# Key scores that follow the next block's queries, lists selected block by block, and keys kept in the place of the probabilities

## The reference

```python
q = (xc @ w_q).reshape(t, PEER_HEADS, 2, PEER_QDIM // 2)          # 1024 -> 2048 = 16 x 128
sc = jnp.einsum('thpc,hpnc->thpn', q, sub_keys)                   # 16 lists of 128 scores for a token
v_half, i_half = lax.top_k(sc, PEER_TOPK_HALF)                    # the best 16 of each list
cand = v_half[:, :, 0, :, None] + v_half[:, :, 1, None, :]        # 8 x 256 sums
top_s, pos = lax.top_k(cand, PEER_TOPK)                           # the best 16 of each: 128 experts a token
g = jax.nn.softmax(top_s, axis=-1)
act = jax.nn.gelu(jnp.einsum('thkd,td->thk', u_tab[expert], xc))
return jnp.einsum('thk,thkd->td', g * act, v_tab[expert])
```

## Time and profile before

| | |
|---|---|
| median of 3 executions | 2381.94 us (2380.4 to 2388.47) |
| profiled execution, its own time | 2383.69 us |
| its span in the profile | 2381.9 us, mean granted PE clock 0.877 |
| PE, DVE, ACT, POOL busy | 1820.2, 1430.4, 806.3, 638.4 us |
| gathers of the four feeds | 512 on POOL, from 222 us on |
| first route, PE | query blocks from 135.5 us |

### The profile page before, as it was taken

How to read it: one execution, slowest core, us unless ns; L and a number is a source line. 1 busy time by engine, 2 the same in 40 slices (tenths; PEclk the granted TensorE clock), 3 DMA queues, 4 the chain that set the end, 5 groups by cost and what they waited for, 6 DMA issues and landing times.

```text
span 2381.9 us, 21120 instructions
## 1 busy us (share of the span) xinstructions
PE 1820.2 (76%) x6754; PEld 1103.0 (46%) x6754; DVE 1430.4 (60%) x2933; ACT 806.3 (34%) x2074; POOL 638.4 (27%) x524
## 2 busy tenths in 40 slices
PE   6586877877777877777787776764786977987988
PEld 3473333623323362232445332653342445866976
DVE  2439845769665567965446896667566144554644
ACT  1211353233334423342432334212654123432532
POOL 0001423435333344443224453424452000000000
PEclk9597988889998998999888898887998975988999
DMA  8067988999999999999879998999896720442442
GB/s 290 20 236 279 406 323 335 419 421 421 378 419 396 338 422 421 406 392 421 320 259 412 420 421 340 421 421 420 341 421 264 252 103 36 177 194 100 178 161 102
DMA packets 106525, 744.79 MB, mean 313 GB/s; under 512 B 12848, under 2 KB 13744, under 8 KB 18352
## 3 DMA queue, kind: packets, MB, share of 16 engines
q0 software_dynamic: 73728, 536.90, 55.3%
q1 hardware_dynamic: 30240, 198.67, 21.8%
q10 hardware_dynamic: 2448, 7.87, 0.9%
HBM read 742.35 MB, written 1.05 MB: 312 GB/s over the span
## 4 chain that ended last, share of the span: by engine, by line
PE 41%; DMA 21%; DVE 21%; ACT 10%; issue 4%; DVEq 1%; POOL 1%; PEldq 1%; POOLq 0%; ACTq 0%; PEld 0%; SPq 0%
DMA sb_work<-in_peer_uv,sb_expert 18%; PE ps_acc L1270 11%; DVE sb_work L1234 6%; PE bank L434 4%; PE bank L1102 4%; PE bank L496 3%; PE bank L497 2%; PE bank L498 2%; PE bank L677 2%; DMA sb_wring<-in_peer_w_q 2%; DVE sb_x L1242 2%; ACT sb_probs L728 2%; PE ps_acc L1659 2%; PE ps_acc L498 1%; PE ps_acc L496 1%
## 5 line engine op out<-in xcount | busy, mean ns | idle before, releaser
L1270 PE MATMUL ps_acc<-sb_work,sb_diag 128*128 128x512 f32 x1532 | 800.3, 670 | 243.4 <-ACT sb_diag L1259 203.6
L2060 POOL DMA_INDIRECT sb_work<-in_peer_uv,sb_expert x512 | 636.0, 1242 | 1175.0 <-PE ps_acc L1270 590.6
L1234 DVE CUSTOM_DVE_ANT_0 sb_work<-sb_work,sb_h 128x1024 f32<-128x1024 f32 x512 | 616.8, 1224 | 203.4 <-DMA sb_work<-in_peer_uv,sb_expert 179.1
L1270 PEld LDWEIGHTS ps_acc<-sb_work,sb_diag 128*128 128x128 f32 x1532 | 308.9, 213 | 681.9 <-issue 671.9
L1250 ACT ACTIVATE sb_dots<-sb_dots 128x1 f32<-128x1 f32 x512 | 102.5, 200 | 626.4 <-DVE sb_dots L1234 597.4
L1242 DVE SCALAR_TENSOR_TENSOR sb_x<-sb_work,sb_weight,sb_x 128x1024 f32<-128x1024 f32 x129 | 165.3, 1281 | 71.4 <-ACT sb_weight L1251 71.2
L490 DVE TENSOR_TENSOR sb_work_r<-sb_wring,sb_work_r 128x2048 fp32r<-128x2048 f32 (+1 forms) x60 | 127.2, 2147 | 85.6 <-ACT sb_work_r L483 85.6
L434 PE MATMUL bank<-sb_wring,sb_hT 128*128 128x512 f32 (+2 forms) x392 | 155.4, 554 | 16.0 <-DMA sb_wring<-in_mla_w_ukv 5.4
L1259 ACT ACTIVATE sb_diag<-sb_ident,sb_weight 128x128 f32<-128x128 f32 x383 | 153.8, 402 | 15.2 <-PE ps_acc L1270 2.7
L1251 ACT ACTIVATE sb_weight<-sb_dots,sb_share 128x1 f32<-128x1 f32 x512 | 150.8, 295 | 16.6
L1102 PE MATMUL bank<-sb_hT,sb_wring 128*128 128x128 f32 x1024 | 127.0, 290 | 19.9 <-DMA sb_wring<-in_peer_w_q 16.9
(11 more groups left out here) (286 smaller groups left out, 2156.5 us busy)
## 6 DMA issues: line engine op xcount, KB each, us to landing
sb_wring<-in_w_mix SPq DMA_DIRECT2D x36, 1024.0 KB, 9.0
sb_wring<-in_peer_w_q SPq DMA_DIRECT2D x32, 1024.0 KB, 7.6
sb_wring<-in_hyb_w_in SPq DMA_DIRECT2D x20, 1024.0 KB, 5.0
sb_wring<-in_w_gate SPq DMA_DIRECT2D x16, 1024.0 KB, 5.5
sb_wring<-in_w_up SPq DMA_DIRECT2D x16, 1024.0 KB, 4.8
sb_wring<-in_w_down SPq DMA_DIRECT2D x16, 1024.0 KB, 4.9
sb_wring<-in_mla_w_uq SPq DMA_DIRECT2D x12, 768.0 KB, 9.4
sb_wring<-in_hyb_w_out SPq DMA_DIRECT2D x8, 1024.0 KB, 5.9
```

What stands on the lines that cost most here:

```text
L1234: e.tensor_tensor_reduce(u, u, h[:, t, :], 1.0, 0.0, ALU.mult, ALU.add, dots[:, i:i + 1]).then_inc(dot_ready, 1)
L1270: last = e.matmul(ps_acc[:, b * 512:(b + 1) * 512], diag[:, number % DIAGS, :], ring[:, n % RING, D + b * 512:D + (b + 1) * 512], start=k ...
L2060: pool.indirect_dma_start(ring[:, n % RING, :], None, a["peer_uv"], bass.IndirectOffsetOnAxis(ap=expert[:, t, n % P:n % P + 1], axis=0)).t ...
```

## The change

- The keys leave the weight stream. They are loaded to `probs` by a DMA of their own (`load_keys`), on SP's queue ahead of the route's first weight piece, after the last attention stage is over on all three engines.
- PE computes the scores of block b behind the queries of block b+1 (`score`), and of the last block at the end. ACT copies them in the same order (`take_scores`). The banks of `products` are handed out in that order.
- DVE selects the 16 lists in four blocks of four, each with its five rounds, as soon as its scores are there. The `made` points stand one before the first block and one ahead of each. The points between the five rounds are gone (5 * [9.0] + [5.0] becomes [9.0]), and the last of `made` states 7.0 for 4.0.
- Where a norm's result is not in place, its squares go to the result's buffer and no longer to `probs`.

```diff
+                    to = squares[t][:, 0:width] if dst is src else dst(t)
...
+        keys = probs[:, :, :, :].rearrange("p a b c -> p (a b c)")
...
+            def load(sp):
+                for e in ("dve", "act", "pe"):
+                    sp.wait_ge(done[e], free_from)
+                sp.dma_start(keys, a["peer_keys"][layer]).then_inc(keys_landed.sem, 16)
...
-            keys = weights(a["peer_keys"][layer], 1, SLOT)
-            key_units = [products.take() for _ in range(4)]
-            given_back[keys] = key_units[-1].full_at()
+                if b:
+                    key_units.append(products.take())
+            key_units.append(products.take())
+            asides[plan[0][0][0][0]] = load_keys(layer, attended[-1])
...
-            made = [point(7.0, "pe") for _ in range(4)] + [point(4.0, "pe")]
-            ranked = [point(us) for us in 5 * [9.0] + [5.0] + 5 * [6.5] + [3.0] + 6 * [4.5]]
+            made = [point(7.0, "pe") for _ in range(4)] + [point(7.0, "pe")]
+            ranked = [point(us) for us in [9.0] + 5 * [6.5] + [3.0] + 6 * [4.5]]
...
+                def score(b):
+                    plan[b][1].wait_emptied(e)
+                    u = key_units[b]
+                    u.wait_free(e)
+                    e.wait_ge(keys_landed.sem, keys_there)
+                    for j in range(4 * b, 4 * b + 4):
+                        last = e.matmul(u.ap[:, (j % 4) * P:(j % 4 + 1) * P], qT[:, j, :],
+                                        keys[:, j * P:(j + 1) * P], start=True, stop=True)
+                    last.then_inc(u.full, 1)
...
                     last.then_inc(u.full, 1)
+                    if b:
+                        score(b - 1)
                     made[b]("pe", e)
...
+                score(3)
...
-                top16(halves, True)
+                made[0]("dve", e)
+                for b in range(4):
+                    made[b + 1]("dve", e)
+                    key_units[b].wait_emptied(e)
+                    top16(halves[4 * b:4 * b + 4])
...
+                if n in asides:
+                    asides[n](sp)
```

More of the change, by code:

```diff
@@ L234, in build @@
         given_back = {}
+        asides = {}
+        attended = []
         ends = {"pe": 0, "act": 0, "dve": 0}
@@ L832, in attend @@
             stage(pe=pe, act=act, dve=dve, points=[p for g in plan for p in g["points"]], us=5.0)
+            attended.append(len(stages))
         raw = sb("raw", [P, 8])
@@ L1105, in pe @@
                     last.then_inc(u.full, 1)
+                    if b:
+                        score(b - 1)
                     made[b]("pe", e)
-                slot_wait(e, keys)
-                for b, u in enumerate(key_units):
-                    plan[b][1].wait_emptied(e)
-                    u.wait_free(e)
-                    for j in range(4 * b, 4 * b + 4):
-                        last = e.matmul(u.ap[:, (j % 4) * P:(j % 4 + 1) * P], qT[:, j, :],
-                                        slot_ap(keys)[:, 0, j * P:(j + 1) * P], start=True, stop=True)
-                    last.then_inc(u.full, 1)
+                score(3)
                 if other:
@@ L1122, in act, with take_scores @@
                     other["first_act"](e)
+                def take_scores(b):
+                    u = key_units[b]
+                    u.wait_full(e)
+                    e.copy(key_scores[:, 4 * b:4 * b + 4, :], u.ap.rearrange("p (n t) -> p n t", n=4)
+                           ).then_inc(u.free, 1)
                 for b, (_, u) in enumerate(plan):
@@ L1125, in act @@
                     e.copy(qT[:, 4 * b:4 * b + 4, :], u.ap.rearrange("p (n t) -> p n t", n=4)).then_inc(u.free, 1)
+                    if b:
+                        take_scores(b - 1)
                     made[b]("act", e)
-                for b, u in enumerate(key_units):
-                    u.wait_full(e)
-                    e.copy(key_scores[:, 4 * b:4 * b + 4, :], u.ap.rearrange("p (n t) -> p n t", n=4)
-                           ).then_inc(u.free, 1)
+                take_scores(3)
                 if other:
@@ L1180, in dve @@
                 cf = key_scores.rearrange("p n k -> p (n k)").rearrange("p (h m) -> p h m", h=EH)
-                top16([(cf[:, j, :], top[:, j, :], top_at[:, j, :].bitcast(U32)) for j in range(EH)], False)
+                top16([(cf[:, j, :], top[:, j, :], top_at[:, j, :].bitcast(U32)) for j in range(EH)], [rest.pop(0) for _ in range(5)])
                 at = top_at.rearrange("p n k -> p (n k)").bitcast(I32)
```

36 lines of the change are left out of this document (18 added, 18 removed).

## The result

The changed kernel takes **2357.47 us** (median of 4, 2355.4 to 2359.07), the kernel before beside it 2382.58 us (4). The ratio is 0.9885, with a 95% interval of 0.9873 to 0.9898: 1.15% faster. I had forecast 2368, a saving of 13.6 us; it is 25 us. The profiled execution has a span of 2353.6 us for 2381.9; it is the fastest of its kernel's four (2355.4), so its 28.3 us of difference are 3.2 more than the 25.1 of the medians. Numbers in brackets behind a median are executions.

What follows compares the result with a forecast made beforehand. The DMA queue was taken as the bound from 222 to 1822 us, DVE as the path before. Terms -7.3 - 7.7 - 4.6 + 6 = -13.6 us gave 2368 us; own range 2360 to 2376, wider 2354 to 2386.

Steps and rivals of the forecast that it cites:

- First route: Ahead of the first gather, where DVE is the path: half the lists hidden under PE's queries, minus 7.3 us.
- Items moved out of the routes: Three feeds: items moved to attention, where the DMA queue has room, gain minus 7.7 us; bounds 0 and 20.
- Handovers: From feed to feed: last gather's slot freed one wide DVE instruction nearer the route's end, twice 2.3, minus 4.6 us.
- Routes under a feed: Three later routes: queue stays the bound, lists not fully covered by the ring of slots cost 2 us each, plus 6.
- Keys, norm, SP's order: Keys ahead of the queries' pieces on SP's queue, norm squares in another buffer, wait for attention's end: no cost.
- Signs: Trace marks: first gather about 215 us, second route 24 shorter, stretches ahead 20 or more longer, DMA share in routes 1.01.
- the standing queue: Rival, routes under a feed: queue stands still during lists, 10 us a route, 2392.3 us; share below 0.97; chance 0.14.
- Only the first route gains: Rival: nothing gained in the feeds, fuller attention stages take as much as they give; 2374.6 us, chance 0.20.
- Free items in attention: Rival: moved items come free in the attention stages, a gain of 20 us; 2350.0 us, chance 0.13.
- POOL beside additions on DVE: Rival: gathers issued beside DVE additions take longer on POOL, 12.6 us if the queue waits; 2380.9 us, chance 0.10.

Runs made afterwards that it cites:

- Experiment 3: Changed kernel's route in the first route alone, the three under a feed as before with its numbers; 2377.54 us, ratio 0.9954 to the kernel before.
- experiment 7: Kernel before, with 8.0 for 6.0 stated at the attention points under a feed, so more items there; 2367.60 us, ratio 0.9926.
- experiment 2: Kernel before with new stated numbers alone: last of made 7.0, five points between rounds 0.8 each, no overlap; 2385.38 us, ratio 0.9997.
- experiment 10: Kernel before, with PE computing each group's scores twice in softmax attention stages, no item moved; 2403.64 us, ratio 1.0083.
- experiment 5: Changed kernel with 8.0 for 6.0 stated at the attention points under a feed; 2340.71 us, ratio 0.9820 to the kernel before.
- experiment 9: Changed kernel with 10.0 for 6.0 stated at the softmax attention points; 2341.12 us, ratio 0.9823 to the kernel before.
- experiment 1: Changed kernel with stated numbers as before, the five 9.0 points in a row behind the four list blocks; 2388.17 us, ratio 1.0019 to the kernel before.
- experiment 8: Changed kernel with stated numbers as before, three 9.0 points between the list blocks, two behind; 2373.25 us, ratio 0.9960 to the kernel before.
- Experiment 4: Changed kernel's place for keys and norm squares, with order and numbers of before, no overlap; 2379.10 us, ratio 0.9977 to the kernel before.

## Why the prediction was right in its sign and small in its size

The measured 2357.5 us lies below the 2360 to 2376 that I had called the forecast's own range, and within the wider 2354 to 2386. The sign is not luck: experiments 3 and 7 each have one of its two gains apart. That the sum is short by 11 us comes from one term; two others were wrong by 3 us each, both to the side of too much gain, and the price that the sum rests on, 2.50 us for a piece, holds: the second route moved 417 x 179.8 = 75.0 MB before, 71.5 pieces, at 2.51 us.

**First route: right.** 8.7 us for 7.3. Of these, 0.7 are not the change's: PE's first query product already stood at 134.77 for 135.47, and in experiments 2 and 7, which change nothing ahead of it, it stands at 134.1 and 134.3. The first three blocks of lists begin at 153.51, 161.67 and 169.75, 1.0, 1.1 and 1.45 us ahead of the forecast. Experiment 3 has the term alone: 9.3 us at the first numbers, 6.1 in the whole.

**Items moved out of the routes: the step that was mis-sized.** I had taken 7.7 us of the 20 that eight items in attention could give, and nothing for the items in the other stretches. The 30 items that left the routes, by their order, are 75 us at 2.50, and the stretches ahead grew by 18.3 + 18.6 + 9.7 = 46.6, so the term measured 28.4. This splits the feeds by items alone, though, and the keys' 1 MB pieces moved as well: that of the second route is now issued at 395.75 us, ahead of the first query product at 438.0, and was issued at 457.35 before, behind the one at 428.4. What the queue moved is a second count, each stretch's GB/s times its length. The stretches ahead have 382, 400 and 378 GB/s for 357, 386 and 354; that is 33.0 MB more, 31.5 pieces, and makes the term 32.1. The routes, at 415, 407 and 398 GB/s for 417, 415 and 416, moved 30.6 pieces less. So either size is good to some 4 us, and no experiment has the term by itself. Two causes, by items:

- In attention the gathers rose by seven, and the stages by 1.4 + 2.2 - 4.6 = -1.0 us: 7 x 2.50 + 1.0 = 18.5. My price, a dot product or 2.2 us of PE in the chain for each item, was too high in the second stage (2.2 us for two items, where I had taken 3.4), far too high in the first (1.4 for three, 6.4 taken for four), and had the wrong sign in the third. The sum took the product's duration at the clock of before as fixed.
- The other stretches took 23 items for 47.6 us, 2.07 each and not 2.50: 9.9 us. A part is room that I hadn't looked for. Before, the share was 0.97 from the first gather to the first attention stage and 0.97 behind it, which at 1.01 is 4.9 us of room in these 122.6 us; in the changed kernel it is 1.00 and 0.99, 1.9 us. The other two feeds have the same shares there before and after, to 0.01, so the rest of the 9.9 stays open:

```profile
213.20:298.50 85.30, 60.30 (x150) 25.62 (x151) 64.09 (x154) 31.26 (x97) 40.16 (x37) 0.89 1.00 411
...
383.80:438.00 54.20, 41.84 (x92) 17.18 (x90) 35.74 (x57) 15.48 (x48) 21.65 (x18) 0.81 0.99 406
```

**The third attention stage** is where the price of an item had the wrong sign. PE's products there, grouped by shape with mean ns of one and the idle time ahead, before:

```profile
L1270 PE MATMUL ps_acc<-sb_work,sb_diag 128*128 128x512 f32 x78 | 45.4, 734 | 7.0 <-ACT sb_diag L1259 7.0
L677 PE MATMUL bank<-sb_work,sb_probsT 128*128 128x64 f32 x64 | 12.6, 378 | 13.4 <-ACT sb_probsT L701 13.4
```

after:

```profile
L1300 PE MATMUL ps_acc<-sb_work,sb_diag 128*128 128x512 f32 x86 | 44.0, 656 | 8.0 <-ACT sb_diag L1289 8.0
L680 PE MATMUL bank<-sb_work,sb_probsT 128*128 128x64 f32 x64 | 9.6, 313 | 11.1 <-ACT sb_probsT L704 11.1
```

and in experiment 10:

```profile
L1271 PE MATMUL ps_acc<-sb_work,sb_diag 128*128 128x512 f32 x78 | 42.5, 692 | 7.0 <-ACT sb_diag L1260 7.0
L655 PE MATMUL ps_scores<-sb_work 96*128 96x256 f32 x64 | 14.5, 380 | 0.3 <-DVEq L276 0.3
```

At 734 ns and the busy time of before, the 86 products would take 45.4 x 86/78 = 50.1 us; they take 44.0. With the 3.0 us of the values, PE is 9.1 us shorter at the higher clock, against 4.7 for the two items; the scores take 1.2 more (8.8 for 7.6), and its waits are 1.3 shorter. Together that is -4.5, of the stage's -4.6. That the items bring the clock, in the old order as in the new, is what experiments 2, 5, 7 and 9 show, in which this stage has 22 to 33 gathers and a clock of 0.89 to 0.95, and experiments 1 and 8, which have 20 and 0.80. Experiment 10 adds PE work and nothing else: the clock rises to 0.87, and the same 78 products take 42.5 for 45.4 us. It gave back 3.5 us of the 6.9 that the second scores cost (14.5 for 7.6). So more PE work can raise the clock by itself, but not in every stage: in the second stage of the same run it fell from 0.92 to 0.88. Why two items gave back more (9.1) is open. PE's waits in the stage are 20.4 us before, 20.4 in experiment 10 and 19.1 with the two items, so it may be where the additions stand; that is argued, not shown. Of this the Trainium skill has a rule, in its page TensorE: Matmul & The Clock Gate, section HAM oscillation — how this bites in real kernels: PE falls back to half rate where its waits are long against its stretches of work. The rows of this stage go the same way (0.80 with 20.4 us of waits, 0.90 with 19.1). The rise to 0.87 in experiment 10, at 20.4 us of waits and more work, does too; the fall in its second stage, at unchanged waits of 14.0 us and more work, doesn't.

**Handovers: wrong.** I had taken 2.3 us off each of the last two. POOL's last gather of a feed and the first of the next, before (second feed) and after (second and third):

```profile
998.13 0.94 POOL L2060 DMA_INDIRECT sb_work<-in_peer_uv,sb_expert  x1 [0.78 <-PE ps_acc L1270]
1013.13 0.94 POOL L2060 DMA_INDIRECT sb_work<-in_peer_uv,sb_expert  x1 [14.06 <-DVE sb_expert L1203]
...
978.38 1.14 POOL L2092 DMA_INDIRECT sb_work<-in_peer_uv,sb_expert  x1 [2.33 <-PE ps_acc L1300]
992.15 0.93 POOL L2092 DMA_INDIRECT sb_work<-in_peer_uv,sb_expert  x1 [12.63 <-DVE sb_expert L1233]
...
1390.93 1.15 POOL L2092 DMA_INDIRECT sb_work<-in_peer_uv,sb_expert  x1 [2.32 <-PE ps_acc L1300]
1404.71 0.93 POOL L2092 DMA_INDIRECT sb_work<-in_peer_uv,sb_expert  x1 [12.63 <-DVE sb_expert L1233]
```

The gap is 13.8 us twice; before it was 15.0 and 14.2. That is 1.6 us and not 4.6. What POOL waited for ahead of a feed's last gather is PE's addition of an item, before as after, and I had priced DVE's place alone.

**Routes under a feed: right, a little low.** 67.7 us less where 75 had left: 7.3 us lost, with the handovers' gain 8.9, for 6 (8.8 and 10.4 by the 30.6 pieces). The share is 1.00, 0.99 and 0.97 for 1.00 in all three before, and the loss stands where I had put it, at the end of the blocks of lists and just behind:

```profile
912.00:932.00 20.00, 14.48 (x26) 5.77 (x25) 19.72 (x58) 6.20 (x21) 9.54 (x8) 0.84 0.88 346
...
1305.00:1325.00 20.00, 3.46 (x25) 2.99 (x24) 19.73 (x61) 4.93 (x16) 6.42 (x5) 0.65 0.89 358
1325.00:1345.00 20.00, 14.42 (x26) 5.77 (x25) 19.72 (x58) 6.05 (x21) 9.41 (x8) 0.84 0.87 336
```

To 1.01 these miss 2.6, 2.4 and 2.8 us, 7.8 in all; in the route from 438 us on no such hole is seen. DVE's waits for gathers in that route fell from 27.2 to 7.4 us:

```profile
DVE sb_work L1264 <- DMA sb_work<-in_peer_uv,sb_expert: 7.4, 12, 1.3
```

With the order alone they are 25.8 (experiment 8), and with the numbers alone 27.5 (experiment 2): it takes both. This is what the overlap is for in a feed: blocks of lists lie where DVE waited for gathers, so the items can go without the gap of experiment 2.

**Keys, norm, SP's order: not shown to be nothing.** Experiment 4 measured 4.6 us where I had none, and left open where. The term's reason, that the keys' 10.39 us ended PE's wait and not that of the queue, fits a profile in which no share changed by more than 0.01, but that profile is of an execution without the gain. The time behind the last gather, 570.7 for 569.0 us, did not get shorter.

**Signs.** Of those that I had named, the first route's came (numbers at 213.2, idle time 14.64), and so did the shorter second route (25.7 us for 24) and the fuller attention stages (0.86 and 0.81). The stretches ahead grew by 18.3, 18.6 and 9.7 us, all less than the 20 us named. The share in the routes is 1.00, 0.99 and 0.97 for the 1.01 named, at its lowest just where I had set the limit for the standing queue. The 560 us behind the last gather were counted from 1822 us; the last gather is issued at 1812.91.

**Rivals.** Only the first route gains: experiments 3 and 8 are near that kernel, at 0.9954 and 0.9960 for the changed kernel's 0.9885. Free items in attention, 2350.0, missed by 7.5 us where the forecast missed by 10.8: its 20 us came as 18.5, though not because items are free but because one stage became shorter; the 9.9 us of the other stretches it hadn't, and it left out the loss in the routes. The standing queue is what experiments 1 and 2 show at 0.83 and 0.57, and the changed kernel has a little of it, at 0.87 to 0.89. POOL beside additions on DVE: a gather takes 66.84 / 50 = 1.34 us on POOL in the second route, for 1.23 before, and the queue is at 1.00 all the same.

## What to carry to other kernels

Where one queue is the bound in most stages, a change pays by moving its work to where the queue has room, and under the full queue of these routes an overlap paid only as far as it let that work go; read the DMA share of every stretch, also of those at 0.97. Two edits can give little by themselves, here 0.4% (experiment 8) and nothing (experiment 2), and 1.15% together, so try the pair. When work is added to a stage in which the granted clock is low, here 0.80, read that clock before pricing the work: the price taken from a trace at that clock had the wrong sign here. And go on until the room is used: here 8.0 for 6.0 gave 0.7% more, 10.0 nothing more.

## What the runs showed of the hardware

A stage became shorter with more work in it: 87.2 us with 20 gathers at a clock of 0.80, 82.6 with 22 at 0.90, and 96.0 with 33 at 0.95 in experiment 9. Products added by themselves raised the clock in that stage as well (0.87), but cost more than they gave back, and in another stage the clock fell with them, from 0.92 to 0.88. How far the rise comes from the work and how far from its place isn't shown.

One core's DMA held 415 to 417 GB/s over a whole route at a share of 1.00 (154.1 to 179.8 us), with gathers of 1 MB.
